# Two rotary turns made by ScalarE copies of shifted rows, another first bank in the output projection, and a second pooled tile begun early

## What is computed

```python
# first block
h = rms_norm(x, norm_pre) * (1 + scale) + shift            # scale, shift from c @ w_ada
xa, ga, q, k, v, gb = split(h @ w_in)                      # six parts of 512 columns
q, k = rotary(q, positions), rotary(k, positions)          # 8 heads of 64; halves of 32 turned against each other
x = x + gate * rms_norm(concat(ya, yb) @ w_out, norm_post) # ya: recurrence, yb: attention
# second block
p = modulate(x, norm1_g, ...) @ w_in_2                     # pool, q, k, v, rwkv, gates
pc = modulate(ctx, norm1_g, ...) @ w_in_2                  # 256 context tokens: only k, v, rwkv are used
q, k = rms_norm(q per 64) * q_norm_g, rms_norm(k per 64) * k_norm_g
q, k = axial_rope(q), axial_rope(k)                        # each half of 32 has its own angle; its halves of 16 are turned
pool = (window_mean(u) - u) @ pool_w * pool_scale          # 4 groups of 128 channels
x = x + mod * mix(pool, diff_attention(q, k, v), rwkv);  x = x + mod * moe(x)   # 32 experts, top 2
# a turn of a pair of halves
rotated = concat([x1 * cos - x2 * sin, x2 * cos + x1 * sin])
```

## Time and profile before

| | |
|---|---|
| median of three runs | 1852.87 us |
| the profiled execution | 1852.16 us |
| its span, first to last instruction | 1850.3 us |
| around the span | 1.9 us |
| mean granted clock of TensorE | 0.97 of full |
| busy shares of the span | TensorE 91%, its weight loads 49%, VectorE 47%, ScalarE 28%, GpSimd 6% |
| DMA | 358 MB, mean 194 GB/s |

### The profile page before, as it was taken

The page is one execution under the profiler, slowest core; times in us unless marked ns, Lnnn a source line. Parts: engine busy times, 40 slices in busy tenths (PEclk is TensorE's granted clock), DMA queues, the critical chain, the costliest instruction groups (busy, mean ns, idle before and its releaser), DMA issues.

```text
span 1850.3 us, 36848 instructions
## 1 busy us (share of the span) xinstructions
PE 1683.9 (91%) x16262; PEld 901.6 (49%) x16262; DVE 862.3 (47%) x1563; ACT 517.9 (28%) x995; POOL 115.8 (6%) x145
## 2 busy tenths in 40 slices
PE   5999999999998999999999999998999978777886
PEld 3444555445546555456667766544553323223332
DVE  3887564547647475446565645253361221212110
ACT  3810443311137321554255431131231100101010
POOL 0000100000000000210000000001000110000001
PEclk9999999999999999999999998999999999999999
DMA  9254634331220130232221210375469999999997
GB/s 395 111 173 160 247 125 153 127 122 46 69 90 1 54 123 1 104 110 72 77 82 50 66 55 21 124 292 208 177 254 423 416 425 415 421 414 425 416 424 278
DMA packets 50613, 358.31 MB, mean 194 GB/s; under 512 B 8405, under 2 KB 8621, under 8 KB 30736
## 3 DMA queue, kind: packets, MB, share of 16 engines
q1 hardware_dynamic: 37232, 307.31, 41.4%
q0 software_dynamic: 13216, 48.59, 8.0%
HBM read 336.61 MB, written 27.36 MB: 197 GB/s over the span
## 4 chain that ended last, share of the span: by engine, by line
PE 70%; DMA 18%; ACT 4%; DVE 4%; issue 2%; SPq 1%; POOL 0%; DVEq 0%; ACTq 0%; POOLq 0%
PE psum L210 67%; DMA arena<-in_w 18%; ACT arena L207 3%; PE psum L213 3%; DVE arena L157 1%; DVE arena L167 1%; SPq L143 1%; DVE arena L183 1%; ACT L207 1%; DVE arena L163 0%; DVE arena L171 0%; DVE arena L175 0%; POOL arena L141 0%; DMA arena<-in_tok 0%; DVE arena L162 0%
## 5 line engine op out<-in xcount | busy, mean ns | idle before, releaser
L210 PE MATMUL psum<-arena 32*32 32x16 f32 (+9 forms) x15618 | 1606.6, 303 | 138.9 <-DMA arena<-in_w 66.3
L210 PEld LDWEIGHTS psum<-arena 32*32 32x32 f32 (+5 forms) x15618 | 832.4, 134 | 861.3 <-issue 748.0
L207 ACT ACTIVATE arena<-psum 128x512 f32<-128x512 f32 (+4 forms) x350 | 174.1, 497 | 833.3 <-PE psum L210 631.5
L157 DVE TENSOR_TENSOR arena<-arena,psum 128x512 f32<-128x512 f32 (+3 forms) x124 | 62.1, 501 | 352.4 <-PE psum L210 204.1
L157 DVE TENSOR_TENSOR arena<-arena 128x512 f32<-128x512 f32 (+8 forms) x311 | 188.9, 607 | 32.5 <-ACT arena L207 16.1
L207 ACT ACTIVATE arena<-arena 128x512 f32<-128x512 f32 (+9 forms) x253 | 139.0, 549 | 201.9 <-DVE arena L183 52.3
L207 ACT ACTIVATE arena<-psum,arena 128x128 f32<-128x128 f32 (+3 forms) x221 | 111.6, 505 | 260.6 <-PE psum L213 135.5
L167 DVE SCALAR_TENSOR_TENSOR arena<-arena 128x512 f32<-128x512 f32 (+7 forms) x236 | 158.9, 673 | 27.7 <-DMA arena<-in_w 10.5
L213 PE MATMUL psum<-arena 128*128 128x128 f32 x644 | 103.7, 290 | 19.5 <-ACT arena L207 11.6
L213 PEld LDWEIGHTS psum<-arena 128*128 128x128 f32 x644 | 73.7, 145 | 78.6 <-issue 54.1
L175 DVE RECIPROCAL arena<-arena 128x1 f32<-128x1 f32 (+4 forms) x69 | 78.7, 1141 | 63.9 <-ACT arena L207 60.4
(11 more groups left out here) (50 smaller groups left out, 186.6 us busy)
## 6 DMA issues: line engine op xcount, KB each, us to landing
arena<-in_w SPq DMA_DIRECT2D x117, 2048.0 KB, 42.3
arena<-in_w SPq DMA_DIRECT2D x24, 1024.0 KB, 12.1
arena<-in_w SPq DMA_DIRECT2D x48, 256.0 KB, 3.1
arena<-kd POOLq DMA_DIRECT2D x28, 256.0 KB, 3.4
gd<-arena SPq DMA_DIRECT2D x24, 256.0 KB, 3.6
arena<-gd SPq DMA_DIRECT2D x24, 256.0 KB, 5.3
arena<-in_w SPq DMA_DIRECT2D x8, 512.0 KB, 11.3
arena<-in_w POOLq DMA_DIRECT2D x8, 512.0 KB, 5.0
```

Of the source, the lines that this page charges most:

```text
L157: return self.ends(self.e.tensor_tensor(out, a, b, op))
L207: return self.ends(self.e.activation(out, a, func, **kw))
L210: return self.ends(self.e.matmul(out, lhs, rhs, start=start, stop=stop))
```

## The change

1. Rotary of the first block. `perm1` matmuls, the copy to `raw` and the tile `rot1` in PSUM go (8 matmuls and 8 VectorE copies). ScalarE instead makes four copies of 32 rows by 512 columns, from PSUM, each into the rows of the other half: `halves_swapped`. VectorE multiplies the PSUM tile by COS, the swapped tile by SIN, and adds.
2. Rotary of the second block. `perm2` matmuls go (8). ScalarE makes four copies of 32 rows from `raw` into the buffer of the squares, one tile after the square root. So that whole groups of 32 rows swap, the host reorders the q and k channels within each head (`ROTATED`: 16-row groups 0, 2, 1, 3), and with them the norm weights and the angle tables.
3. `out1` starts the ring at bank 1, where it would stand at bank 2.
4. `("pool", 0)` and `("pool", 1)` are both begun over three row blocks before `h2(3)`; their last 128 columns follow in `proj2`.

```diff
 def proj1_tensor():
-    def rotate(c, m):
-        yield
-        T.wait_ge(V["raw1", c, m], *ps.take(ALL8, "rot1", c, m))
-        T.mm(ps["rot1", c, m], C["perm1"], tm[m % 2], True, True).then_inc("rot1", c, m)
...
+def halves_swapped(out, in_):
+    for q in range(4):
+        last = A.act(out[32 * q:32 * q + 32], in_[32 * (q ^ 1):32 * (q ^ 1) + 32], ACT.Copy)
+    return last
 def proj1_scalar():
+        elif c in (8, 9):
+            A.wait_ge(T["p1", c, m])
+            if (c, m) > (8, 1):
+                A.wait_ge(V["rope1", c, m - 2] if m > 1 else V["rope1", 8, m + 2])
+            halves_swapped(tm[m % 2], b).then_inc("rot1", c, m)
 def proj1_vector():
     def rotate(c, m):
-        V.wait_ge(T["p1", c, m])
-        V.cp(raw, b).then_inc("raw1", c, m)
-        ps.free(V.last(), "p1", c, m)
         yield
-        V.tt(o, raw, COS, ALU.mult)
-        V.wait_ge(T["rot1", c, m])
-        V.tt(tmp, ps["rot1", c, m], SIN, ALU.mult)
-        ps.free(V.last(), "rot1", c, m)
-        V.tt(o, o, tmp, ALU.add).then_inc("rope1", c, m)
+        V.wait_ge(A["rot1", c, m])
+        V.tt(o, ps["p1", c, m], COS, ALU.mult)
+        ps.free(V.last(), "p1", c, m)
+        V.tt(turned_, turned_, SIN, ALU.mult)
+        V.tt(o, o, turned_, ALU.add).then_inc("rope1", c, m)
 def out1_tensor():
+    ps.turn[ALL8] = 1
...
-    T.wait_ge(W.landed(26), A["f2", 2, 0], V["f2", 2, 1], *ps.take(ALL8, "p2", "pool", 0))
-    for k in range(8):
-        T.mm(ps["p2", "pool", 0][:, 0:384], wk(26)[:, k, c4(0)], HT[:, k, 0:384], k == 0, k == 7)
+    T.wait_ge(W.landed(26), A["f2", 2, 0], V["f2", 2, 1])
+    for m in range(2):
+        T.wait_ge(*ps.take(ALL8, "p2", "pool", m))
+        for k in range(8):
+            T.mm(ps["p2", "pool", m][:, 0:384], wk(26)[:, k, c4(m)], HT[:, k, 0:384], k == 0, k == 7)
 def proj2_tensor():            # normed
-        if n != "kc":
-            yield
-            T.wait_ge(V["nrm", n, m], *ps.take(ALL8, "rot2", n, m))
-            T.mm(ps["rot2", n, m], C["perm2"], raw_of[n](m), True, True).then_inc("rot2", n, m)
...
-        if (n, m) != ("pool", 0):
+        begun = n == "pool" and m < 2
+        if not begun:
             T.wait_ge(W.landed(c), *ps.take(ALL8, "p2", n, m))
...
-            if (n, m) == ("pool", 0):
+            if begun:
                 T.mm(b[:, 384:512], w[:, k, c4(m)], HT[:, k, 384:512], k == 0, k == 7)
 def proj2_scalar():            # normed, behind the square root
+        if n != "kc":
+            yield
+            A.wait_ge(V["nrm", n, m])
+            halves_swapped(sq_of[n](m), raw_of[n](m)).then_inc("rot2", n, m)
 def proj2_vector():            # normed
-        V.wait_ge(T["rot2", n, m])
-        V.tt(sq, ps["rot2", n, m], RP["sin2"], ALU.mult)
-        ps.free(V.last(), "rot2", n, m)
+        V.wait_ge(A["rot2", n, m])
+        V.tt(sq, sq, RP["sin2"], ALU.mult)
+ROTATED = np.r_[0:16, 32:48, 16:32, 48:64]   # host: w_in_2 columns 512:1536, qn, kn, rope tables
```

More of the change, by code:

```diff
@@ L796, in proj1_tensor @@
         def proj1_tensor():
-            def rotate(c, m):
-                yield
-                T.wait_ge(V["raw1", c, m], *ps.take(ALL8, "rot1", c, m))
-                T.mm(ps["rot1", c, m], C["perm1"], tm[m % 2], True, True).then_inc("rot1", c, m)
-            late = Late()
             for t, (c, m) in enumerate(PROJ1):
@@ L815, in proj1_tensor @@
                     T.mark("w", c)
-                late.add(rotate(c, m) if c in (8, 9) else iter(()))
                 lru_tensor(t)
@@ L819, in proj1_tensor @@
                     ada_tensor(ADA_SUMS["p1", t], ALL8)
-            late.drain()
+        def halves_swapped(out, in_):
+            for q in range(4):
+                last = A.act(out[32 * q:32 * q + 32], in_[32 * (q ^ 1):32 * (q ^ 1) + 32], ACT.Copy)
+            return last
         def proj1_scalar():
@@ L845, in rotate @@
             def rotate(c, m):
-                o, raw, tmp = (QT if c == 8 else KT)[:, m, :], tm[m % 2], tm[2]
-                b = ps["p1", c, m]
-                V.wait_ge(T["p1", c, m])
-                V.cp(raw, b).then_inc("raw1", c, m)
+                o, turned_ = (QT if c == 8 else KT)[:, m, :], tm[m % 2]
+                yield
+                V.wait_ge(A["rot1", c, m])
+                V.tt(o, ps["p1", c, m], COS, ALU.mult)
                 ps.free(V.last(), "p1", c, m)
-                yield
-                V.tt(o, raw, COS, ALU.mult)
-                V.wait_ge(T["rot1", c, m])
-                V.tt(tmp, ps["rot1", c, m], SIN, ALU.mult)
-                ps.free(V.last(), "rot1", c, m)
-                V.tt(o, o, tmp, ALU.add).then_inc("rope1", c, m)
+                V.tt(turned_, turned_, SIN, ALU.mult)
+                V.tt(o, o, turned_, ALU.add).then_inc("rope1", c, m)
             V.ts(lw[0], P["lam"], -1.0, None, ALU.mult)
@@ L3111, in cut @@
         return [w[:, j * n:(j + 1) * n].reshape(k, 128, n).transpose(1, 0, 2).reshape(128, k * n) for j in range(c // n)]
-    w2 = i["w_in_2"][0]
+    w2 = i["w_in_2"][0].copy()
+    w2[:, 512:1536] = w2[:, 512:1536].reshape(1024, 16, 64)[:, :, ROTATED].reshape(1024, 1024)
     mid = np.zeros((1024, 512), np.float32)
@@ L3141, in params @@
         "conv_b": col(i["conv_b"]), "b_a": col(i["b_rg_a"]), "b_x": col(i["b_rg_x"]), "lam": col(i["lru_lambda"]),
-        "norm_rec": col(i["norm_rec"]), "qn": col(np.tile(i["q_norm_g_2"][0], 2)), "kn": col(np.tile(i["k_norm_g_2"][0], 2)),
+        "norm_rec": col(i["norm_rec"]), "qn": col(np.tile(i["q_norm_g_2"][0][ROTATED], 2)), "kn": col(np.tile(i["k_norm_g_2"][0][ROTATED], 2)),
         "mu0": col(turned(i["shift_mu_2"][0, 0])), "mu1": col(turned(i["shift_mu_2"][0, 1])), "w0": col(i["decay_w0_2"][0]),
@@ L3208, in rope_constants @@
     p = np.arange(128)
+    p = p // 64 * 64 + ROTATED[p % 64]
     pos = np.where(((p % 64) < 32)[:, None], rows[None], cols[None])
```

## The result

| | before | after |
|---|---|---|
| median | 1852.73 us (4 runs) | 1836.44 us (4 runs, 1834.11 to 1838.63) |
| ratio to before, 95% interval | | 0.9913 [0.9895, 0.9931] |
| profiled execution | 1852.16 us | 1838.63 us |
| its span | 1850.3 us | 1836.8 us |
| mean granted clock | 0.97 | 0.968 |

Forecast was 1832.6 us. The measured time is 3.8 us above it, inside the range. The gain is 16.3 us by the medians and 13.5 us by the two profiled executions, where 20.3 us was forecast.

What follows compares the result with a forecast made beforehand. TensorE was taken as the bound ahead of the experts, whose DMA-limited weight stream moves with it. Gains of 6.9 + 5.8 + 5.3 + 2.3 = 20.3 us took 1852.16 to 1831.9, median 1832.6; range 1826 to 1842.5 us.

Steps and rivals of the forecast that it cites:

- Part 1: In `proj1`, eight matmuls of 0.86 us removed from TensorE's path: gain 6.9 us.
- The cover of the squares: In `proj1`, the `lru_scalar` squares behind tile (8, 0)'s copies end 1.7 us before TensorE wants them.
- Part 2: In `out1`, the first bank shifted: `mix(1, 1)` starts 4.0 us earlier and runs 1.8 us shorter, gain 5.8 us.
- Rival E: In `out1`, another owner holds bank 4, so the bank shift gains nothing: 1838 us; chance 0.04.
- Part 3: `out1` to `proj2`: second pooled tile begun early fills idle time ahead of the turn of `h2(3)`; gain 5.3 us.
- the open choice: Passage to `proj2`: full clock assumed; if it stayed at 0.50, the tails would take twice as long, 2.5 us less gain.
- Part 4: In `proj2`, 8.4 us from `rot2` matmuls and a wait, minus 3.3, 1.7 and 1.1: gain 2.3 us.
- the loop: In `proj2` q tiles, VectorE and ScalarE wait on each other: 8.35 us a tile, where TensorE needs 7.73.
- A: The ScalarE copies cost more; at 1.08 us each, `proj2` loses 7.5 us: 1842.4 us; chance 0.10.
- B: Slower: the VectorE-ScalarE loop in `proj2` becomes the bound; at 2 us a copy about 1869 us; chance 0.04.
- C: No loop in `proj2`: copies at 0.5 us or less, or idle time not lowering the clock; 1826 to 1831 us; chance 0.14.
- D: The experts' weight stream, at the DMA limit, swallows the gain: about 1852 us; chance 0.04.

Runs made afterwards that it cites:

- the run with the edges: Changed kernel with two of four `proj2` copies moved to VectorE, and only the edges of `PP` zeroed; 1830.63 us, ratio 0.9868.
- 2.27 alone: Kernel before with only the second block's rotary changed (ScalarE copies in `proj2` for the `rot2` matmuls); 1848.40 us, ratio 0.9979.
- Taking the loop away: Changed kernel with two of the four `proj2` copies made by ScalarE and the other two by VectorE; 1824.82 us, ratio 0.9858.
- the run with the doubled copies: Changed kernel with each of ScalarE's four `rot2` copies in `proj2` made twice; 1849.97 us, ratio 0.9988.
- part 2 alone: Kernel before with only the ring started at bank 1 in `out1`; 1842.29 us, ratio 0.9945.
- before again: Kernel before, unchanged, profiled a second time; 1851.60 us.
- four matmuls more: Changed kernel with four more 128x512 matmuls at tile v 5, their result overwritten; 1838.57 us, one run.

## Why the prediction came out as it did

**The gain up to the last v tile, 20.3 us: 19.84 measured.** Part 1: 6.9 against 6.87, from 8 x 0.86, with no idle time on TensorE. The cover of the squares held: the copies of tile (8, 0) ended at 111.05, the squares at 113.76, and the next tile's copies started at 115.48 behind TensorE, so 1.7 us were left, as worked out.

Part 2: 5.8 against 5.79. Both halves came true, though shared a little otherwise: without the 4.03 us of idle time `mix(1, 1)` starts 4.20 us earlier after attention (37.12 us behind it instead of 41.32), and its row is 1.60 us shorter at clock 1.00 (7.03 instead of 8.63), where 4.0 + 1.8 had been worked out. Rival E is out.

Part 3: 5.3 against 5.0. The turn of `h2(3)` ran right behind the two sets, and the clock stayed at 1.00, which was the open choice. The two tails took 3.81 us and not 2 x 1.79 = 3.58, and the wait ahead of `pw(0)` was 1.40 and not 1.7; together these cancel, and from the first set to `pw(0)` it is 17.52 us (350.71 to 368.23), where 17.5 had been worked out (362.60 to 380.1). The missing 0.3 is a slip in the base: the working set the end of `pw(0)` on TensorE against 386.36, which it had formed from the start of a ScalarE copy. In the kernel after, that copy starts at 376.26, 0.30 us behind the point at which `pw(0)` and the tile behind it are through by the same working (368.23 + 0.86 + 6.87 = 375.96). The prediction gave the zeroing of `PP` as the head of that wait. It stands in the chain, but the run with the edges shows that the tail of pool 0 holds the copy just as long; of the zeroing only 0.09 us counts.

Part 4: 2.3 against 2.08 (2.27 alone). Every term has its row: reciprocals 8.33 us apart (8.35 forecast), the wait behind kc 1 at 3.26 us (3.3), clock 0.63 behind it (a fall was chosen over none), the wait for `ada_tensor(16)` at 1.25 us (1.1). Taking the loop away gave 5.15 us back, where the two terms of wait and clock were 3.3 + 1.7 = 5.0; a little of the 5.15 comes from v 2, where the wait fell from 1.25 to 0.97 us.

**The price of a copy.** 0.655 us was taken from the squares of the earlier trace rows; measured are 2.60 / 4 = 0.65 from SBUF and 2.44 / 4 = 0.61 from PSUM. So four copies of 32 shifted rows take what four squares of 128 unshifted rows do, and the condition of rivals A and B (a penalty for crossing rows) does not show. The Trainium skill, "ScalarE: Activation LUTs", section "What ACT_TABLE_LOAD costs", gives 186 ns and 0.833 ns a column, an estimate of 0.61 us for 512 columns; its overlap of about 93 ns between activations would have made it 0.52. The copies from PSUM agree with the first figure, those from SBUF are 0.04 us above it, and neither shows the overlap where each copy waits for the one before. The Trainium skill's "VectorE: DVE Perf Modes", section "The TRN2 errata — SBUF-src ops pay a fixed extra latency per instruction", has ScalarE 52 cycles, 43 ns, slower from SBUF than from PSUM; the two prices here differ by 0.04 us, so on that the trace agrees.

**Rivals.** C, no loop, fell: the wait was there with its clock. D, swallowed by the weight stream, fell: the end from the first expert on took 553.0 to 554.8 us in all twelve profiles, whether the first expert started at 1265.78 or 1302.50 us. The stream moves as a whole, as the earlier trace rows said. A and B did not come to pass with a copy of 0.65, and the run with the doubled copies confirms their arithmetic as far as c = 1.31: at 2 us for each tenth up to 1.0 and 2.8 above, the step from 0.655 comes to 15.6 us, and 16.8 were measured.

**The term that was mis-sized** is the last one, that ahead of the experts each microsecond saved arrives at the end, so that every landmark from `diff` on comes about 20 us earlier. The last part of the way holds, as the twelve ends show; the stretch between has its own length in each execution, and that error is not in the sum. The first expert started 13.0 us earlier in the profiled execution of after and 19.3 in the second. The 3.8 us between the forecast and the measured median are of this size: eleven executions of the changed program lie between 1830.9 and 1850.3 us with a median of 1834.83, and 50 of the kernel before between 1847.31 and 1863.07 with 1852.80. That is a gain of 18.0 us, with 19.84 read from the stages. What of the last 1.8 us is scatter and what a loss is open. That the median of the first four executions came out within 4 us of the forecast is in part luck: executions of one program lie up to 19 us apart. The working took one profile of before as exact behind `diff`; a second profile of before alone would have moved that base by 2.4 us in the stretch and by 2 us in attention.

## What to carry to other kernels

Cost an edit by the stage it is in, between two landmarks that both versions share: here the edited stages repeat to a few tenths of a microsecond, while whole executions of one program scatter by ten or more, and the medians of the four parts added up to half as much again as the stages. Before giving an unexplained microsecond in untouched code to the change, profile the same program twice and compare TensorE's busy time for the same instruction count, and the granted clock; where both differ and the other engines' busy times agree, it is the clock. When a step moves from one engine to another that feeds it back, write the loop out as a sum (here 5.7 us + 4 copies) and compare it with the pace of TensorE; where it is over that pace, share the moved work between the two engines, as this made 5.15 us.

## What the runs showed of the hardware

- The same program spends different amounts of time at half clock: 45.4 and 59.2 us (after), 34.1 and 46.2 (before) in the same stretch, worth 0.37 us each. Over twelve profiles of nearly the same code it was 27.3 to 69.9 us.
- Attention takes 83.5 to 84.3 us in eight profiles, with 3.4 us at half clock, and 85.2 to 85.5 us in four (part 2 alone, the edges, before again, four matmuls more), with 6.8 us at half clock, in unchanged code.
- VectorE copies 32 x 512 from SBUF to SBUF in 0.44 us (0.88 for two), where ScalarE takes 0.65.
- A 128 x 512 reciprocal takes 3.35 us, 4.9 times a product of the same shape (0.69), and is what makes VectorE the slow side of the loop.
